# The window-state copies of a two-layer decoder step: from GpSimd's queue in joined rows to ScalarE's queue in rows of at most 2 KB

## What is computed

```python
def even_layer(x, ...):             # layer 0: differential attention (A) and indexer-sparse attention (B)
    z = rmsnorm(x, pre_w) @ w_in    # 1024 x 3652
    ...                             # attention over own rows (prompt) or paged caches (samples)
    return x + rmsnorm(mix @ w_out, post_w), (ka, va, kb, vb, ki)

def odd_layer(x, ...):              # layer 1: native sparse attention (C) and dilated attention (D)
    parts = rmsnorm(x, pre_w) @ w_in            # 1024 x 6924
    kw_all = concatenate([s_wk, kwin], axis=1)  # window state of the samples, and the new row
    kd_all = [concatenate([d_bufs[2 * g], kd[g]], axis=1) for g in range(3)]
    ...
    keep = lambda a, w: a[:, a.shape[1] - min(w, a.shape[1]):]
    d_new = [keep(kd_all[g], w), keep(vd_all[g], w)]     # for the windows w = 128, 512, 2048
    return y, (..., keep(kw_all, 512), keep(vw_all, 512), *d_new)
```

| state | copies | rows copied | bytes of one copy | MB of all |
|---|---|---|---|---|
| `d_k2`, `d_v2` | 16 | 1024 of 2 KB | 2,097,152 | 33.6 |
| `d_k1`, `d_v1` | 16 | 511 of 2 KB | 1,046,528 | 16.7 |
| `d_k0`, `d_v0` | 16 | 127 of 2 KB | 260,096 | 4.2 |
| `c_win_k`, `c_win_v` | 16 | 511 of 512 B | 261,632 | 4.2 |

## Time and profile before

### The profile page before, as it was taken

How to read it: one execution, slowest core, us unless ns; L and a number is a source line. 1 busy time by engine, 2 the same in 40 slices (tenths; PEclk the granted TensorE clock), 3 DMA queues, 4 the chain that set the end, 5 groups by cost and what they waited for, 6 DMA issues and landing times.

```text
span 806.2 us, 12528 instructions
## 1 busy us (share of the span) xinstructions
PE 721.1 (89%) x4785; PEld 386.0 (48%) x4785; DVE 409.8 (51%) x1052; ACT 220.4 (27%) x620; POOL 163.2 (20%) x202
## 2 busy tenths in 40 slices
PE   6587999898999999998999898899995989999896
PEld 4355545444554334333544544555553445664543
DVE  3113698999976973524243233354748324331214
ACT  6143113234112300014153423122421024232222
POOL 0513311112330235420110130422231001001000
PEclk9988999999999999989999999799998889999999
DMA  8644798689994878895885495778699957757801
GB/s 295 209 152 135 289 384 330 247 291 329 362 359 153 311 234 274 304 392 197 275 292 193 137 368 188 261 300 332 226 356 388 401 190 300 279 174 293 315 4 55
DMA packets 67827, 213.09 MB, mean 264 GB/s; under 512 B 5056, under 2 KB 28784, under 8 KB 61880
## 3 DMA queue, kind: packets, MB, share of 16 engines
q0 software_dynamic: 20320, 142.55, 48.3%
q1 hardware_dynamic: 47288, 69.64, 25.2%
q10 hardware_dynamic: 160, 0.11, 0.0%
HBM read 206.24 MB, written 64.68 MB: 336 GB/s over the span
## 4 chain that ended last, share of the span: by engine, by line
PE 63%; DVE 18%; DMA 7%; ACT 4%; issue 4%; another core or an unknown queue 2%; DVEq 0%; SPq 0%; ACTq 0%
PE psum L941 28%; PE psum L1007 10%; DMA ring<-in_w_in_odd 5%; PE psum L952 5%; PE psum L871 4%; DVE SA L2434 4%; PE psum L1096 3%; PE psum L922 2%; DVE ring L2431 2%; PE psum L1062 2%; PE psum L1329 2%; DVE PD L2431 1%; PE psum L1250 1%; PE psum L1192 1%
## 5 line engine op out<-in xcount | busy, mean ns | idle before, releaser
L941 PE MATMUL psum<-ring,XB 128*128 128x512 f32 (+3 forms) x760 | 332.5, 591 | 13.4 <-DMA ring<-in_w_in_odd 11.1
L941 PEld LDWEIGHTS psum<-ring,XB 128*128 128x128 f32 x760 | 145.1, 196 | 173.4 <-issue 157.9
L1007 PE MATMUL psum<-Z,ring 128*128 128x512 f32 x256 | 118.6, 609 | 1.5 <-issue 1.2
L1007 PEld LDWEIGHTS psum<-Z,ring 128*128 128x128 f32 x256 | 47.2, 193 | 62.8 <-issue 61.8
L1902 DVE TENSOR_TENSOR RT<-Z,const 128x128 f32<-128x128 f32 (+6 forms) x43 | 11.5, 267 | 123.4 <-ACT Z L1563 92.8
L1563 ACT ACTIVATE Z<-psum,stat 128x512 f32<-128x512 f32 (+3 forms) x38 | 24.1, 634 | 170.6 <-PE psum L941 165.1
L952 PE MATMUL psum<-ring,XB 128*8 128x128 f32 (+3 forms) x1664 | 51.9, 268 | 8.6 <-issue 7.1
L952 PEld LDWEIGHTS psum<-ring,XB 128*8 128x8 f32 x1664 | 42.1, 90 | 28.3 <-issue 27.1
L1727 ACT ACTIVATE SM<-SM,stat 128x128 f32<-128x128 f32 (+4 forms) x56 | 26.9, 480 | 76.9 <-DVE stat L2091 75.8
L1585 ACT COPY Z<-psum 8x128 f32<-8x128 f32 (+3 forms) x104 | 26.1, 251 | 45.8 <-PE psum L952 29.9
L922 PE MATMUL psum<-ring,XB 128*128 128x512 f32 (+1 forms) x72 | 32.1, 594 | 2.6 <-DMA ring<-in_w_in_even 1.5
(11 more groups left out here) (382 smaller groups left out, 901.0 us busy)
## 6 DMA issues: line engine op xcount, KB each, us to landing
ring<-in_w_in_odd SPq DMA_DIRECT2D x9, 2048.0 KB, 14.5
ring<-in_w_in_even SPq DMA_DIRECT2D x6, 2048.0 KB
ring<-in_cmp_w SPq DMA_DIRECT2D x4, 2048.0 KB
ring<-in_w_in_odd SPq DMA_DIRECT2D x8, 1024.0 KB
out_s_d_k<-in_state_d_k POOLq DMA_DIRECT2D x8, 1022.0 KB
out_s_d_v<-in_state_d_v POOLq DMA_DIRECT2D x8, 1022.0 KB
Z<-in_cmp_w POOLq DMA_DIRECT2D x5, 1024.0 KB
ring<-in_state_d_v POOLq DMA_DIRECT2D x5, 1024.0 KB, 7.3
```

The costliest lines, as they stand in the source:

```text
L941: last = mm(out[:, 0:n], xT[:, k, t * 128:(t + 1) * 128], w[:, k * n:(k + 1) * n], start=k == 0, stop=k == KT - 1)
L1007: last = mm(out[:, h * 512:(h + 1) * 512], w[:, (r % 16) * CH + h * 128:(r % 16) * CH + h * 128 + 128], rowsT[:, at:at + 512], start=r == ...
```

## The change

The 64 copies leave GpSimd's stream and go to ScalarE's. ScalarE lists its own events of `ORDER`, from the event `("cache", 0, 6)` in layer 0 to the event `("probs", 29)`, the last attention unit of layer 1, and issues copies behind them so that their number grows in proportion to the events done. The order of the copies is as before. Each is now cut by `PIECES` into `apart` x `rows` x `m` elements: the outer dimension steps by one row of `m`, the middle one by `apart` rows. Neighbours in memory are thus never neighbours in the innermost two dimensions, and the builder can't join them.

```diff
+MOVES_SPAN = (("cache", 0, 6), ("probs", 29))
...
         def moved(name, n):
             src, dst = ins["state_" + name], outs["s_" + name]
             old, new = src.shape[2], dst.shape[2]
-            pieces = next(k for k in range(1, new) if (new - 1) % k == 0 and (new - 1) // k * n <= PART)
-            m = (new - 1) // pieces * n
-            return [(bass.AP(dst.tensor, dst.offset + b * new * n, [[m, pieces], [1, m]]),
-                     bass.AP(src.tensor, src.offset + (b * old + old - new + 1) * n, [[m, pieces], [1, m]]))
+            apart, rows, m = PIECES[new - 1, n]
+            return [(bass.AP(dst.tensor, dst.offset + b * new * n, [[m, apart], [apart * m, rows], [1, m]]),
+                     bass.AP(src.tensor, src.offset + (b * old + old - new + 1) * n, [[m, apart], [apart * m, rows], [1, m]]))
                     for b in range(NB)]
 
+        PIECES = {(1024, 512): (2, 512, 512), (511, 512): (7, 73, 512), (127, 512): (2, 127, 256), (511, 128): (2, 73, 448)}
...
-        MOVED_AFTER = dict(ak=1, ck=1, cv=1, dk=1, wk=1, wv=2, ak0_0=0, ak0_1=0, rows1_2=4, av7_1=3, bv_1=3, bv_3=4,
-                           ck1_1=2, dk0_0=2, dk0_1=2, wk0_1=2, dk2_0=4, dk1_0=2, dk1_1=2, dv0_0=2, dv0_1=2)
...
-            for event in ORDER:
-                if event[0] in stages:
-                    stages[event[0]](*event[1:])
+            own_events = [event for event in ORDER if event[0] in stages]
+            first, last = (own_events.index(event) for event in MOVES_SPAN)
+            moves = list(MOVES)
+            for at, event in enumerate(own_events):
+                stages[event[0]](*event[1:])
+                while first <= at <= last and len(MOVES) - len(moves) < (at + 1 - first) * len(MOVES) // (last + 1 - first):
+                    dst, src = moves.pop(0)
+                    eng.dma_start(dst, src).then_inc(sem("moved"), 16)
...
             pool.wait_ge(sem("index"), 5)
-            moves = list(MOVES)
             for name, queue, parts in items:
                 if queue == "pool":
                     stream(pool, name, parts)
-                    for _ in range(MOVED_AFTER.get(name, MOVED_AFTER.get(name[:2], 0))):
...
-            for dst, src in moves:
-                pool.dma_start(dst, src).then_inc(sem("moved"), 16)
```

## The result

| | before | after |
|---|---|---|
| median of the runs, us | 808.85 (806.92 to 812.52, 4 runs) | 1409.76 (1406.87 to 1411.34, 4 runs) |
| ratio to before | 1 | 1.7415, 95% interval 1.7352 to 1.7479 |
| span of the profiled execution, us | 806.2 | 1407.2 |
| mean granted clock in it, share of full speed | 0.954 | 0.764 |

The kernel takes 74% longer.

The account below looks back on a forecast made before the run. The two DMA engines shared by the two-row copies were taken to bound it: 101 us before the first copy, 970 of copies and 358 of other work make 1429, with 1.9 around the span 1430 us; range 1300 to 1620.

Parts of the forecast that it names:

- Two engines: State copies on ScalarE's queue: a transfer spreads over its outer rows, so three copies of each four run on 2 engines, `d_1` on 7.
- The rival in between: State copies: two-engine copies lie on varying engines or split further; with 4 engines 990 us; chance 0.08.
- 970 us of copies: Packet time of all `d_2`, `d_0`, `d_1` and `c_win` copies on each of the two busiest DMA engines: 970 us.
- 358 us of the others: Weights, gathers and results on each DMA engine from 101 us on: 358 us, taken between 339 and 374.
- The sum: Busiest two engines: 101 us before the first copy, 970 of copies and 358 of other work make 1429 us.
- ScalarE's hold: ScalarE's issue of each `d_2` copy: stands still 32 us until some 383 packets are done, 16 times, 515 us.
- the weights' third: Other work on the same engines during ScalarE's holds: a third of 358 us, raising the compute's end from 1308 to 1427.
- One engine after the other: ScalarE's queue: the two engines' packets are handed out in turn, holding 64 us per `d_2` copy; 1850 us, chance 0.12.
- Sixteen engines: State copies: they spread over all 16 engines after all, giving a faster kernel of 790 us; chance 0.10.
- the 13 us of the earlier trace: TensorE's loss from 613 to 653 us around layer 1's weight load, given back by a mere change of the packets: some 13 us.

## Why the prediction was right, step by step

- **Two engines.** Shown: the packets of q10, 2.1 engines busy when it runs alone, and the series over 2, 4 and 16 outer rows. The Trainium skill's rule ("DMA: Bandwidth & Descriptors", section "Why a DMA increments its semaphore by 16 and not by 1") held in its part on the number of engines; that successive copies share engines is what the 57.5 us per group says. The rival in between, with four engines or changing ones, is refuted by the same numbers.
- **970 us of copies.** Measured 920. The count of packets was right, their time 5% too long: from HBM to HBM, with nothing beside it, a 2 KB packet followed the last after 80 ns, where the loads to SBUF in the earlier trace rows have 84 (573 packets in 3 us on 16 engines). Packets of one engine overlap in both: each took 84 ns here and 88 ns there (104.7%), so overlap isn't what makes the difference, and its cause is open. At least HBM to HBM costs a packet no more than HBM to SBUF.
- **358 us of the others.** From 101 to 1372 us the engines were busy for 0.42 x 1271 = 534 us on average; less the copies' 11.0% of 1407.2, 155 us, that is 379. These shares add up packets that overlap; with that 5% off it is 361.
- **The sum.** 101 + 920 + 361 = 1382, against 1372.1, where q10's last packet ends. That the two engines set the pace is seen directly: cut into pieces of 2 us, the stretch from 101 to 1372 us has only some 36 us in which q10 moved less than four packets. To this the 35 us of compute behind it come: the prediction had set them level and left this out. So 1430 is 1.4% above 1409.76: one term was 50 us too large, and an end of 35 us was missing. That they nearly cancel is luck; the mechanism is not.
- **ScalarE's hold.** Right in size and count (16, around 30 to 57 us), wrong in its mechanism. I had read the earlier trace rows as some 130 descriptors that can wait, and put the hold at the `d_2` copy, 32 us. In truth 13 of the 16 `d_2` copies, 513 per engine, were taken in 0.6 to 0.8 us (the three others in 5.7 to 13.2), and it was the next issue that stood, 667 us in all rather than 515, or 634 with the weights' third. When the first of these holds ended, at 152.04 us, q10 had moved 824 of the 1024 packets. Some 100 were left on each engine, near the 130 that were read from the earlier trace rows; what was wrong is which issue has to wait. The earlier trace rows fits this too: two large loads in 1.04 us, and the one behind held.
- **TensorE's clock**, which no term had. The granted clock fell from 0.97 in the longest stretch of the earlier trace rows to 0.75 here, midway between its two levels of 1.2 and 2.4 GHz. From 140 to 152 us, late in the first hold, TensorE ran nothing and the clock was 0.50, the lower level. PE is busy for 764.9 instead of 721.1 us. It isn't needed to explain the end, since the engines' sum gives that without it.
- **One engine after the other** (1850 us): refuted by the 2.1 engines and by the time. So is what stood beside it, that a held ScalarE holds SyncE: SyncE at 121.53 us, within ScalarE's hold of 114.58 to 152.04, was issued in 0.37 us.

```profile
121.53 0.37 SPq L830 DMA_DIRECT2D ring<-in_w_in_even  x1
```

  The Trainium skill's lock on the generator ("Perfetto Trace Analysis", section "DMA Instruction — HWDGE (DVE, Sync)") is not seen here: whatever it does, a ScalarE held at an issue does not hold SyncE by it.
- **Sixteen engines** (790 us, faster): the rival's size was wrong, which no part of the forecast needed. It took the 13 us of the earlier trace rows for a matter of the packets' length, and 16 KB rows at the same places don't give them back (1.0008). More likely they come from bunched copies, which isn't shown apart; and spreading them evenly costs about as much in layer 0.

## What to carry to other kernels

Before you cut a DRAM-to-DRAM copy, look at the outermost dimension of its pattern: with 2, 4, 7 and 16 on ScalarE's queue it was the number of DMA engines that worked. Once the copies fill them, the end is the sum of packets on the busiest engine, not the bytes over sixteen. A queue that holds its sequencer at an issue while the mean DMA share is low is the sign of it; the instruction that waits is the one behind the large transfer. Bulk copies with no due time belong where the gathers are not late; here that was 0.9935 of before instead of 1.0043, on the same queue and with the same rows, though on two chips.

## What was not expected of the hardware

- ScalarE's queue took a transfer of 1024 packets, 512 on each of two engines, in 0.62 to 0.76 us (13 of 16 times), and held the next issue for up to 57.28 us.
- On one engine packets of 2 KB from HBM to HBM follow each other every 80 ns, though each takes 84.
- At the same places of GpSimd's queue 2 KB rows cost 5.0% (1.0457 to 1.0545) and 16 KB rows nothing that could be measured (0.9973 to 1.0043); on ScalarE's queue at other places 2 KB rows cost 1.0% against joined ones (1.0138 to 1.0043). On GpSimd's queue the 2 KB rows came in packets of 4.7 KB on average, on ScalarE's one by one. The cause of the difference is open.
